# Block sums of a seven-product matmul: from DMAs that add to VectorE with rows loaded aside

## The chip, the cores and the metric

The kernel runs on one core of a Trainium2 chip. The metric is device time in microseconds of one launch. The kernel before took 3009.37 us, the median of three runs (3009.07 to 3009.42).

## The reference, cut to what matters

The program is two transformer blocks in a row, all in fp32, on one sequence of 1024 tokens and a width of 1024. The change touches the last matmul of the first block and what lies beside it:

```python
        gate, up = jnp.split(xn @ w_gate_up[l], 2, axis=-1)
        x = x + (jax.nn.silu(gate) * up) @ w_down[l]
    return rms_norm(x, final_norm_g)
```

`silu(gate) * up` is called h here: 1024 tokens by 2816. `w_down` is 2816 by 1024. Behind it come the norm and the second block, whose context tokens `ctx` (256 by 1024) are normed and modulated on their own.

## The kernel before, in words

Every engine has its own list of instructions, written out in order by a Python function per engine and stage (`down_pe`, `down_act`, `down_dve`, `down_sp`, `down_pool`); each engine works its list strictly in order. `Engine.wait_ge` puts a semaphore wait in front of the next instruction, `did` and `landed` name the event of an instruction or a DMA. The wait holds everything behind it on that engine. SP issues plain loads on its own queue; POOL issues stores, loads and the DMAs that add (`dma_add`), on another queue.

The down product is cut into 2 by 2 blocks and computed with seven block products instead of eight. Names: A is h (`h_dram`, written by the stage before, transposed), A11 to A22 its four blocks, the second digit the half of the inner dimension; B11 to B22 are the blocks of `w_down`. The sums are S1 = A21 + A22, S2 = S1 - A11, S3 = A11 - A21, S4 = A12 - S2, T1 = B12 - B11, T2 = B22 - T1, T3 = B22 - B12, T4 = T2 - B21, up to signs that the results take account of. In the code T1 holds B11 - B12, T2 adds B22 to its source, and so on. `DN_ORDER` is the order of the products: P1 (A11, B11), P2 (A12, B21), P5 (S1, T1), P6 (S2, T2), P7 (S3, T3), P4 (A22, T4), P3 (S4, B22).

Each product has 11 steps, one for each 128 rows of the inner 1408. Step n = 11 * (place in the order) + t runs from 0 to 76 (`dn_step`). A step takes one 128x512 row of A and one of B. ACT writes the rounded high part of each (`dn_highs`), DVE the rest as low part (`dn_lows`), into a ring of four (`hs`, `ws`); ACT waits for PE's step n - 4 before it writes that of step n. PE then does 4 token tiles times 3 matmuls (high-high, high-low, low-high), 12 matmuls of 512 columns, and waits only for the lows of B.

Where the operands of a step lie: for P1, P2, P7 (and A of P4) in rings of eight 128x512 slots, one for A and one for B (`h_slot`, `w_slot`), loaded by SP's `h_ring_load` and `w_ring_load` in the order of use, each waiting until the lows of the slot's user before are made. For P5, P6, P3 and P4's B they lie in two resident buffers of eleven rows, `s_all` (starts as A21) and `t_all` (starts as B12). The block sums turn these in place, S1 to S2 to S4 and T1 to T2 to T4. Here they are all made by DMAs on POOL's queue that add rows from HBM onto what lies in SBUF (`dn_add`), in chunks of 4, 4 and 3 rows; where the sign must turn, ACT first negates the chunk (`dn_negate`). S3 and T3 are made the same way inside the rings, in chunks of 2, 4, 2, 2 and 1 rows. ACT's copies of a step wait for the landing of the add.

Beside this the stage brings back the residual x1 (two halves of the first 512 tokens, then the last 512 tokens, onto `x2`), loads two rows of modulation for the context, loads and norms `ctx` (ACT's squares at step 36, DVE's scaling at step 39, POOL's shift), and DVE adds the products into `x2` (`dn_result`) at the steps that `results` names. `dU2` holds a partial result from step 13 on; `dU3` is free until step 57, but for one row that is scratch of the context's squares. The first transposes of the context (`turn4`) follow step 70 on PE.

## Time and profile before

| | us |
|---|---|
| median of three runs | 3009.37 |
| the profiled execution, its own time | 3012.62 |
| its span, first to last instruction | 3010.80 |
| PE busy | 2828.3 |
| DVE busy | 1795.0 |
| ACT busy | 1352.6 |
| POOL busy | 552.8 |

The profile is of one execution. PE is TensorE's matmuls, PEld its weight loads, DVE is VectorE, ACT ScalarE, POOL GpSimd, SP the engine that issues loads. A row of a timeline is a start, a duration, the engine, the source line (a helper's, the same for many operations), the operation with its operands, how often in a row, and in brackets the idle time before it with what ended it. A window gives busy time and count of each engine, then the granted clock of PE (1.00 is 2.4 GHz, 0.50 is 1.2 GHz), the mean share of the 16 DMA engines, and the rate in GB/s.

### The profile page before, as it was taken

The page shows a single profiled execution, that of the slowest core. Times are in us where ns is not written, and L with a number is a line of the kernel's source. Part 1 is how long each engine was busy: PE and PEld are TensorE (multiplying, and loading weights), DVE is VectorE, ACT ScalarE, POOL GpSimd, SP SyncE. Part 2 cuts the span into 40 slices and gives each one's busy share as a digit, 9 for nine tenths or more (in the row PEclk, how much of TensorE's full clock was granted, in tenths as well). Part 3 has the DMA queues.
Part 4 walks back from the last instruction along what each step waited for, and adds up shares of the span by engine and source line. Part 5 has one row for each costly group of instructions (what it writes and reads, how often), then busy time and mean ns, then how long its engine had stood idle before and what let it go on. Part 6 is the DMA issues. An engine that isn't in the chain of part 4 may idle for free.

```text
span 3010.8 us, 34923 instructions
## 1 busy us (share of the span) xinstructions
PE 2828.3 (94%) x13918; PEld 2247.4 (75%) x13918; DVE 1795.0 (60%) x2506; ACT 1352.6 (45%) x1952; POOL 552.8 (18%) x454
## 2 busy tenths in 40 slices
PE   6999998999999977999999999999999579999997
PEld 5777776788778866888888676666888458888885
DVE  4344534788775446653323555554355669999997
ACT  4344433333333553321111666665213357777775
POOL 0011102555554140332000111111000200000000
PEclk8999999999999988999999999999999789999998
DMA  3210131345654996141221111114324559999996
GB/s 106 84 43 29 43 105 70 99 133 159 184 154 146 309 248 157 39 130 42 68 66 36 49 40 43 39 41 149 105 98 169 223 212 385 398 393 396 397 396 242
DMA packets 258071, 468.65 MB, mean 156 GB/s; under 512 B 28989, under 2 KB 135621, under 8 KB 257397
## 3 DMA queue, kind: packets, MB, share of 16 engines
q1 hardware_dynamic: 223888, 365.46, 34.8%
q0 software_dynamic: 33872, 100.92, 11.6%
q8 instruction: 110, 1.80, 0.3%
q14 instruction: 53, 0.43, 0.0%
q10 hardware_dynamic: 148, 0.04, 0.0%
HBM read 412.79 MB, written 53.58 MB: 155 GB/s over the span
## 4 chain that ended last, share of the span: by engine, by line
PE 85%; DVE 6%; DMA 4%; ACT 3%; issue 2%; POOL 1%; ACTq 0%; POOLq 0%; DVEq 0%
PE PS L130 80%; PE PS L133 5%; DVE m L139 3%; ACT m L136 2%; DMA m<-in_w_down_dram 2%; DVE m L145 1%; DMA m<-h_scratch 1%; DMA m<-in_ctx_dram 1%; ACT L136 0%; DVE m L181 0%; POOL m L139 0%; DVE m L184 0%; DVE m L178 0%; DVE m L148 0%; DMA m<-xh_scratch,small 0%
## 5 line engine op out<-in xcount | busy, mean ns | idle before, releaser
L130 PE MATMUL PS<-m,m 128*128 128x512 f32 (+6 forms) x12102 | 2642.2, 391 | 76.9 <-DVE m L139 55.3
L130 PEld LDWEIGHTS PS<-m,m 128*128 128x128 f32 (+3 forms) x12102 | 2043.7, 185 | 600.2 <-issue 121.3
L136 ACT ACTIVATE m<-m 128x512 fp32r<-128x512 f32 (+5 forms) x739 | 756.4, 1048 | 833.0 <-PE PS L130 402.5
L139 DVE TENSOR_TENSOR m<-m,m 128x512 fp32r<-128x512 f32 (+5 forms) x697 | 882.1, 1292 | 328.7 <-ACT m L136 298.8
L136 ACT ACTIVATE m<-PS 128x512 f32<-128x512 f32 (+4 forms) x507 | 281.9, 578 | 525.7 <-PE PS L130 346.1
L139 DVE TENSOR_TENSOR m<-PS,m 128x512 fp32r<-128x512 f32 (+1 forms) x356 | 233.1, 683 | 346.7 <-PE PS L130 303.7
L139 POOL TENSOR_TENSOR m<-m,m 128x512 f32<-128x512 f32 (+3 forms) x166 | 268.2, 1618 | 584.8 <-DVE small L148 207.9
L133 PE MATMUL PS<-ident,m 128*128 128x128 f32 x1592 | 225.6, 281 | 83.2 <-DVE m L154 36.0
L133 PEld LDWEIGHTS PS<-ident,m 128*128 128x128 f32 x1592 | 193.7, 145 | 122.0 <-DVE m L154 36.2
L136 ACT ACTIVATE m<-m,small 128x640 f32<-128x640 f32 (+4 forms) x199 | 156.3, 788 | 221.1 <-DVE small L142 155.5
L148 DVE CUSTOM_DVE_ANT_0 m<-PS,m 128x640 f32<-128x640 f32 (+4 forms) x192 | 146.4, 775 | 118.6 <-PE PS L130 118.6
L154 DVE COPY m<-PS 128x512 f32<-128x512 f32 (+1 forms) x176 | 106.9, 617 | 134.6 <-PE PS L133 105.8
L145 DVE SCALAR_TENSOR_TENSOR m<-m,small,m 128x512 f32<-128x512 f32 (+1 forms) x155 | 158.5, 1051 | 1.7
L136 ACT ACT_TABLE_LOAD x90 | 115.5, 1283 | 5.5 <-issue 4.0
L145 DVE SCALAR_TENSOR_TENSOR m<-m,vecT,m 128x512 fp32r<-128x512 f32 (+3 forms) x96 | 63.1, 712 | 47.5 <-ACT m L136 46.7
L139 POOL TENSOR_TENSOR m<-m 128x512 f32<-128x512 f32 x52 | 74.8, 1442 | 28.5 <-DMA m<-in_w_gate_up_dram 18.6
L193 POOL DMA_INDIRECT m<-xh_scratch,small x16 | 19.8, 1238 | 304.9 <-PE PS L133 285.3
L193 POOL DMA_INDIRECT xa_scratch<-m,small x15 | 25.5, 1698 | 217.4 <-DVE m L145 217.4
L136 ACT ACTIVATE m<-m,vecT 128x512 fp32r<-128x512 f32 (+2 forms) x80 | 41.2, 598 | 47.2 <-PE PS L130 47.2
L187 POOL DMA_DIRECT2D y_scratch<-m x8 | 4.3, 533 | 259.7 <-DVE m L139 259.7
L139 POOL TENSOR_TENSOR m<-ident,small 128x1024 f32<-128x1024 f32 x16 | 43.3, 2707 | 33.5 <-DVE small L160 33.5
L139 DVE TENSOR_TENSOR small<-small 128x8 f32<-128x8 f32 (+4 forms) x49 | 7.7, 160 | 68.9 <-ACT small L136 63.9
(82 smaller groups left out, 516.5 us busy)
## 6 DMA issues: line engine op xcount, KB each, us to landing
m<-in_w_exp_gate_dram SPq DMA_DIRECT2D x64, 1024.0 KB, 9.2
m<-in_w_exp_up_dram SPq DMA_DIRECT2D x64, 1024.0 KB, 9.3
m<-in_w_exp_down_dram SPq DMA_DIRECT2D x64, 1024.0 KB, 8.8
m<-in_w_mod_dram SPq DMA_DIRECT2D x48, 512.0 KB, 3.8
m<-in_w_gate_up_dram SPq DMA_DIRECT2D x44, 512.0 KB, 6.5
m<-in_w_in_dram SPq DMA_DIRECT2D x41, 512.0 KB, 4.1
m<-in_w_in_dram SPq DMA_DIRECT2D x12, 1024.0 KB, 5.1
h_scratch<-m POOLq DMA_DIRECT2D x22, 512.0 KB, 3.5
```

Of the source, the lines that this page charges most:

```text
L130: return Unsent() if self.e is None else self.e.matmul(o, l, r, start=first, stop=last, **k)
L133: return Unsent() if self.e is None else self.e.transpose(o, i, ident)
L136: return Unsent() if self.e is None else self.e.activation(o, i, fn, **k)
L139: return Unsent() if self.e is None else self.e.tensor_tensor(o, a, b, op)
L145: return Unsent() if self.e is None else self.e.scalar_tensor_tensor(out=o, in0=a, scalar=s, in1=b, op0=op0, op1=op1)
L148: return Unsent() if self.e is None else self.e.tensor_tensor_reduce(**k)
L154: return Unsent() if self.e is None else self.e.tensor_copy(o, i)
L187: return Unsent() if self.e is None else self.e.dma_start(o, i)
L193: return Unsent() if self.e is None else self.e.indirect_dma_start(*a, **k)
```

## The change

Five of the eight sums (T1, S1, S2, S3, T3) are made by DVE, in chunks of 4, 4 and 3 rows, one instruction each (`dn_sum`), at the steps that the new table `sums` names. T1 takes B11 from the ring, where it lies for P1. The other four take their second operand from `dU3`, into which SP loads four rows at a time (`aside_load`, twelve loads); each load waits for the sum before it. The rings hold A11 and B22 for P7 instead of A21 and B12, and from ring entry 22 on the slots are counted two further, so that a chunk of four lies in slots 0 to 3 or 4 to 7. The B ring's loads that overwrite P1's rows wait for T1's sum. T2, T4 and S4 stay DMAs that add. The residual's last part goes to the end of POOL's adds, and its landings are told apart as "first", "second" and "last": `U2_in` waits for "second", `U3_in` and `U3_in0` for "last". The squares' scratch moves from `dU3` to `ar(94, 512)`, with a wait for T3's first sum.

```diff
@@ -1529,15 +1528,20 @@
         dU2, dU3 = ar(134, 4, 512), ar(86, 4, 512)
-        H_RING = [("P1", t, "A11", None) for t in range(11)] + [("P2", t, "A12", None) for t in range(11)] + [
-            ("P7", t, "A21", "A11") for t in range(11)] + [("P4", t, "A22", None) for t in range(11)]
-        W_RING = [("P1", t, "B11", None) for t in range(11)] + [("P2", t, "B21", None) for t in range(11)] + [
-            ("P7", t, "B12", "B22") for t in range(11)]
-
+        H_RING = [(P, t, b) for P, b in (("P1", "A11"), ("P2", "A12"), ("P7", "A11"), ("P4", "A22")) for t in range(11)]
+        W_RING = [(P, t, b) for P, b in (("P1", "B11"), ("P2", "B21"), ("P7", "B22")) for t in range(11)]
         CHUNKS = [(0, 4), (4, 4), (8, 3)]
-        RING_CHUNKS = [(0, 2), (2, 4), (6, 2), (8, 2), (10, 1)]
-        H_AT = {(P, t): j for j, (P, t, b, added) in enumerate(H_RING)}
-        W_AT = {(P, t): j for j, (P, t, b, added) in enumerate(W_RING)}
+
+        def ring_slot(j):
+            return (j if j < 22 else j + 2) % 8
+
+        def ring_before(j):
+
+            users = [i for i in range(j) if ring_slot(i) == ring_slot(j)]
+            return users[-1] if users else None
+
+        H_AT = {(P, t): j for j, (P, t, b) in enumerate(H_RING)}
+        W_AT = {(P, t): j for j, (P, t, b) in enumerate(W_RING)}
         def dn_step(P, t):
             return 11 * DN_ORDER.index(P) + t
@@ -1554,18 +1558,32 @@
             return v.rearrange("(t p) n -> p t n", p=128)
         def h_ring_load(sp, j):
-            P, t, b, _ = H_RING[j]
+            (P, t, b), s_ = H_RING[j], ring_slot(j)
             c = t + 11 * (b[2] == "2")
             sp.wait_ge(f"h_st{c % 2}", c)
-            if j >= 8:
-                sp.wait_ge("h_low", dn_step(*H_RING[j - 8][0:2]), "A")
-            sp.dma_start(h_slot[j % 8], h_block(b, t, 1)).then_inc(*sp.landed(f"h_in{j % 8}", "d", j))
+            if ring_before(j) is not None:
+                sp.wait_ge("h_low", dn_step(*H_RING[ring_before(j)][0:2]), "A")
+            sp.dma_start(h_slot[s_], h_block(b, t, 1)).then_inc(*sp.landed(f"h_in{s_}", "d", j))
         def w_ring_load(sp, j):
-            P, t, b, _ = W_RING[j]
-            if j >= 8:
-                sp.wait_ge("h_low", dn_step(*W_RING[j - 8][0:2]), "B")
-            sp.dma_start(w_slot[j % 8], w_block(b, t, 1)).then_inc(*sp.landed(f"wd_in{j % 8}", "d", j))
+            (P, t, b), s_ = W_RING[j], ring_slot(j)
+            if ring_before(j) is not None:
+                P_, t_, _ = W_RING[ring_before(j)]
+                sp.wait_ge("h_low", dn_step(P_, t_), "B")
+                if P_ == "P1":
+                    sp.wait_ge("x2_half", "T1", t_ // 4)
+            sp.dma_start(w_slot[s_], w_block(b, t, 1)).then_inc(*sp.landed(f"wd_in{s_}", "d", j))
+
+
+        ASIDE = [("S1", 0), ("S1", 1), ("S1", 2), ("S3", 0), ("T3", 0), ("S2", 0), ("S2", 1), ("S2", 2),
+                 ("S3", 1), ("T3", 1), ("S3", 2), ("T3", 2)]
+
+        def aside_load(sp, S, c):
+            n, (t0, m) = ASIDE.index((S, c)), CHUNKS[c]
+            if n:
+                sp.wait_ge("x2_half", *ASIDE[n - 1])
+            src = w_block("B12", t0, m) if S == "T3" else h_block({"S1": "A22", "S2": "A11", "S3": "A21"}[S], t0, m)
+            sp.dma_start(dU3[:, 0:m, :], blocks(src)).then_inc(*sp.landed("cs_raw", S, c))
         def w_last_load(sp, t):
...
@@ -1595,17 +1613,34 @@
             sp.wait_ge("gu_acc", 21, "P7")
             sp.dma_start(t_all, blocks(w_block("B12", 0, 11))).then_inc(*sp.landed("ct_in"))
             for j in range(8, 22):
-                if j == 12:
+                if j == 11:
                     sp.wait_ge("gu_acc", 21, "P4")
                     sp.wait_ge("gu_up", 21, "C12")
                     sp.wait_ge("h_st0", 20)
                     sp.wait_ge("h_st1", 21)
                     sp.dma_start(s_all, blocks(h_block("A21", 0, 11))).then_inc(*sp.landed("cs_raw"))
+                if j in (14, 20):
+                    aside_load(sp, "S1", (14, 20).index(j))
                 h_ring_load(sp, j)
                 w_ring_load(sp, j)
-            for j in range(22, 33):
+            aside_load(sp, "S1", 2)
+            for j in range(22, 26):
                 h_ring_load(sp, j)
                 w_ring_load(sp, j)
+            aside_load(sp, "S3", 0)
+            for j in range(26, 30):
+                h_ring_load(sp, j)
+                w_ring_load(sp, j)
+            aside_load(sp, "T3", 0)
+            for c in range(3):
+                aside_load(sp, "S2", c)
+            aside_load(sp, "S3", 1)
+            aside_load(sp, "T3", 1)
+            aside_load(sp, "S3", 2)
+            for j in range(30, 33):
+                h_ring_load(sp, j)
+                w_ring_load(sp, j)
+            aside_load(sp, "T3", 2)
             for t in range(11):
                 h_ring_load(sp, H_AT["P4", t])
             for t in range(4):
...
@@ -1754,25 +1788,39 @@
                 else:
                     dve.tensor_tensor(L, dn_source(n, x)[0], H.bitcast(F32), ALU.subtract).then_inc(*dve.did("h_low", n, x))
-        def ring_rows(S, c):
-
-            t0, m = RING_CHUNKS[c]
-            ring, at_, sem = (h_ring, H_AT, "h_in") if S == "S3" else (w_ring, W_AT, "wd_in")
-            j = at_["P7", t0]
-            return ring(j % 8, m), [(f"{sem}{(j + a) % 8}", "d", j + a) for a in range(m)]
-
-        def dn_negate(act, S, c):
-
-            if S in ("S3", "T3"):
-                v, ready = ring_rows(S, c)
+        def ring_rows(at_, P, ring, sem, c):
+
+            t0, m = CHUNKS[c]
+            js = [at_[P, t0 + a] for a in range(m)]
+            return ring(ring_slot(js[0]), m), [(f"{sem}{ring_slot(j)}", "d", j) for j in js]
+
+        def dn_sum(dve, S, c):
+
+            t0, m = CHUNKS[c]
+            sv, tv, aside = s_all[:, t0:t0 + m, :], t_all[:, t0:t0 + m, :], dU3[:, 0:m, :]
+            if S == "T1":
+                v, ready = ring_rows(W_AT, "P1", w_ring, "wd_in", c)
+                out_, a, b, op = tv, v, tv, ALU.subtract
+                ready.append(("ct_in",))
+            elif S == "S1":
+                out_, a, b, op, ready = sv, sv, aside, ALU.add, []
+            elif S == "S2":
+                out_, a, b, op, ready = sv, aside, sv, ALU.subtract, [("h_low", dn_step("P5", t0 + m - 1), "A")]
             else:
-                t0, m = CHUNKS[c]
-                v = (s_all if S == "S2" else t_all)[:, t0:t0 + m, :]
-                ready = [{"T1": ("ct_in",), "S2": ("h_low", dn_step("P5", t0 + m - 1), "A"),
-                          "T4": ("h_low", dn_step("P6", t0 + m - 1), "B")}[S]]
+                v, ready = ring_rows(H_AT, "P7", h_ring, "h_in", c) if S == "S3" else ring_rows(W_AT, "P7", w_ring, "wd_in", c)
+                out_, a, b, op = v, v, aside, ALU.subtract
             for event in ready:
-                act.wait_ge(*event)
-            act.activation(v, v, ACT.Copy, scale=-1.0).then_inc(*act.did("dn_neg", S, c))
+                dve.wait_ge(*event)
+            if S != "T1":
+                dve.wait_ge("cs_raw", S, c)
+            dve.tensor_tensor(out_, a, b, op).then_inc(*dve.did("x2_half", S, c))
+
+        def dn_negate(act, c):
+
+            t0, m = CHUNKS[c]
+            v = t_all[:, t0:t0 + m, :]
+            act.wait_ge("h_low", dn_step("P6", t0 + m - 1), "B")
+            act.activation(v, v, ACT.Copy, scale=-1.0).then_inc(*act.did("dn_neg", "T4", c))
         SQ_ORDER = [(0, i) for i in range(4)] + [(1, i) for i in range(4, 8)] + [(0, i) for i in range(4, 8)] + [(1, i) for i in range(4)]
...
@@ -1792,18 +1840,8 @@
         def down_act(act):
             for n in range(4, 77):
                 dn_highs(act, n)
-                if n in (5, 6, 7):
-                    dn_negate(act, "T1", n - 5)
-                if n in (27, 31, 34):
-                    dn_negate(act, "S2", (27, 31, 34).index(n))
                 if n in (38, 42, 45):
-                    dn_negate(act, "T4", (38, 42, 45).index(n))
-                if n in (29, 30, 32):
-                    dn_negate(act, "S3", (29, 30, 32).index(n))
-                    dn_negate(act, "T3", (29, 30, 32).index(n))
-                if n in (47, 48):
-                    dn_negate(act, "S3", n - 44)
-                    dn_negate(act, "T3", n - 44)
+                    dn_negate(act, (38, 42, 45).index(n))
                 if n == 50:
                     w_high(act, W_K2)
                 if n == 13:
@@ -1814,9 +1852,10 @@
                     dn_squares(act, 0, (n - 26, n - 25))
                 if n == 36:
                     act.wait_ge("cx_in")
+                    act.wait_ge("x2_half", "T3", 0)
                     for a in range(2):
                         for z in range(2):
-                            square(act, cx[:, a, half512(z)], ssqc[:, a, z:z + 1], "cx", a, z, junk=dU3[:, 0, :])
+                            square(act, cx[:, a, half512(z)], ssqc[:, a, z:z + 1], "cx", a, z, junk=ar(94, 512))
                 if n == 38:
                     root_of(act, ssumc, "cx")
                 if n in (63, 65):
...
+            sums = {4: ("T1", 0), 5: ("T1", 1), 11: ("T1", 2), 12: ("S1", 0), 15: ("S1", 1), 18: ("S1", 2), 23: ("S3", 0),
+                    25: ("T3", 0), 28: ("S2", 0), 31: ("S2", 1), 34: ("S2", 2), 37: ("S3", 1), 40: ("T3", 1), 48: ("S3", 2), 50: ("T3", 2)}
...
@@ -2035,40 +2068,31 @@
             pool.dma_add(v, blocks(src)).then_inc(*pool.landed(*event))
         def down_pool(pool):
-            pool.wait_ge("h_low", 10, "B")
-            for c in range(3):
-                dn_add(pool, "T1", c)
-                dn_add(pool, "S1", c)
-                if c == 0:
-                    pool.dma_start(x2[:, 0:4, 0:512], x1_dram[0:512, 0:512].rearrange("(i p) n -> p i n", p=128)).then_inc(
-                        *pool.landed("x1_back", "first"))
-            pool.wait_ge("h_low", 22, "B")
+            pool.wait_ge("h_low", 12, "B")
+            pool.dma_start(x2[:, 0:4, 0:512], x1_dram[0:512, 0:512].rearrange("(i p) n -> p i n", p=128)).then_inc(
+                *pool.landed("x1_back", "first"))
             pool.wait_ge("sqrow_a")
+            pool.wait_ge("h_low", 18, "B")
             for dst, j, c in ((cA1row, 1, 1), (csh1row, 1, 0)):
                 row_load(pool, dst, j, c, "crows_in")
-            for c in range(3):
-                dn_add(pool, "T2", c)
-                dn_add(pool, "S2", c)
             pool.wait_ge("x1_back", "first")
             pool.dma_start(cx, ctx_2[0].rearrange("(i p) n -> p i n", p=128)).then_inc(*pool.landed("cx_in"))
             for c in range(3):
-                dn_add(pool, "S3", c)
-                dn_add(pool, "T3", c)
+                dn_add(pool, "T2", c)
             pool.wait_ge("cx_in")
             pool.dma_start(x2[:, 0:4, 512:1024], x1_dram[0:512, 512:1024].rearrange("(i p) n -> p i n", p=128)).then_inc(
-                *pool.landed("x1_back"))
-            pool.dma_start(x2[:, 4:8, :], x1_dram[512:1024, :].rearrange("(i p) n -> p i n", p=128)).then_inc(
-                *pool.landed("x1_back", "last"))
+                *pool.landed("x1_back", "second"))
             for c in range(3):
-                dn_add(pool, "S4", c)
                 dn_add(pool, "T4", c)
                 if c == 0:
                     for a in range(2):
                         pool.wait_ge("cx_scaled", a)
                         pool.tensor_tensor(cx[:, a, :], cx[:, a, :], csh1row, ALU.add).then_inc(*pool.did("cx_shifted", a))
-            for c in (3, 4):
-                dn_add(pool, "S3", c)
-                dn_add(pool, "T3", c)
+            for c in range(3):
+                dn_add(pool, "S4", c)
+            pool.wait_ge("x1_back", "second")
+            pool.dma_start(x2[:, 4:8, :], x1_dram[512:1024, :].rearrange("(i p) n -> p i n", p=128)).then_inc(
+                *pool.landed("x1_back", "last"))
             pool.wait_ge("x2_half", "U3", 3)
             pool.dma_start(sqB, rows_dram[1, 2560:3072].partition_broadcast(128)).then_inc(*pool.landed("sqrow_b"))
             pool.wait_ge("h_low", dn_step("P4", 10), "B")
```

## Rows read from the trace of the kernel before

**Rows 1.** The page: busy time by engine, and the chain by engine.
```profile
PE 2828.3 (94%) x13918; PEld 2247.4 (75%) x13918; DVE 1795.0 (60%) x2506; ACT 1352.6 (45%) x1952; POOL 552.8 (18%) x454
...
PE 85%; DVE 6%; DMA 4%; ACT 3%; issue 2%; POOL 1%; ACTq 0%; POOLq 0%; DVEq 0%
```

**Rows 2.** The chain in order of time: start, us, what.
```profile
1005.41 22.99 DMA m<-in_w_down_dram
...
1121.77 31.50 DMA m<-in_w_down_dram
...
1165.51 43.77 PE PS L130 x192
```

**Rows 3.** Timeline of PE, 965 to 1215: start, us, group, idle time before it.
```profile
970.79 54.65 PE L130 MATMUL PS<-m,m 128*128 128x512 f32 x240 [1.40 <-DVE m L139]
1025.64 3.01 PE L130 MATMUL PS<-m,m 128*128 128x512 f32 x12 [0.20 <-DVE m L139]
1029.83 33.26 PE L130 MATMUL PS<-m,m 128*128 128x512 f32 x144 [1.17 <-DVE m L139]
1066.08 12.81 PE L130 MATMUL PS<-m,m 128*128 128x512 f32 x48 [2.99 <-DVE m L139]
1089.20 11.01 PE L130 MATMUL PS<-m,m 128*128 128x512 f32 x36 [10.31 <-DVE m L139]
1102.76 33.32 PE L130 MATMUL PS<-m,m 128*128 128x512 f32 x144 [2.54 <-DVE m L139]
1154.70 54.58 PE L130 MATMUL PS<-m,m 128*128 128x512 f32 x228 [18.63 <-DVE m L139]
1209.12 0.60 PE L133 MATMUL PS<-ident,m 128*128 128x128 f32 x4
```

**Rows 4.** Timeline of ACT, 1170 to 1179: two splits with nothing late.
```profile
1171.29 1.15 ACT L136 ACTIVATE m<-m 128x512 fp32r<-128x512 f32 x2 [1.57 <-PE PS L130]
1174.01 1.16 ACT L136 ACTIVATE m<-m 128x512 fp32r<-128x512 f32 x2 [1.57 <-PE PS L130]
```

**Rows 5.** Windows of 5 us, then the stage: busy by engine, PEclk, DMA share, GB/s.
```profile
1145.00:1150.00 5.00, 0.00 (x0) 0.00 (x0) 0.00 (x0) 0.00 (x0) 0.00 (x0) 0.50 1.13 207
...
985.00:990.00 5.00, 5.00 (x24) 4.14 (x23) 2.50 (x4) 5.00 (x6) 0.00 (x0) 1.00 1.05 388
1030.00:1035.00 5.00, 5.00 (x23) 4.12 (x24) 5.00 (x9) 3.33 (x7) 1.16 (x2) 1.00 1.10 257
970.00:1210.00 240.00, 203.21 (x858) 164.68 (x859) 129.54 (x212) 122.36 (x201) 51.29 (x43) 0.92 0.93 240
```

**Rows 6.** DMA issues in narrow windows, then the page: KB each, us to landing.
```profile
m<-h_scratch SPq DMA_DIRECT2D x1, 256.0 KB, 3.0
...
m<-in_w_down_dram SPq DMA_DIRECT2D x1, 2816.0 KB, 16.4
...
m<-in_w_down_dram SPq DMA_DIRECT2D x1, 256.0 KB, 22.5
...
m<-in_w_in_dram SPq DMA_DIRECT2D x12, 1024.0 KB, 5.1
```

**Rows 7.** Timeline of SP's queue near 1002: one issue and how long it took.
```profile
1001.73 1.87 SPq L187 DMA_DIRECT2D m<-in_w_down_dram  x1
```

**Rows 8.** Timeline of ACT, 1055 to 1090: its wait ahead of the context's squares.
```profile
1084.32 0.63 ACT L136 ACTIVATE m<-m 128x512 f32<-128x512 f32 x1 [14.60 <-DMA m<-in_ctx_dram]
```

**Rows 9.** Timeline of ACT and of DVE, 970 to 1000: splits and the first negation.
```profile
976.58 1.15 ACT L136 ACTIVATE m<-m 128x512 fp32r<-128x512 f32 x2 [1.57 <-PE PS L130]
982.45 10.30 ACT L136 ACTIVATE m<-m 128x2048 f32<-128x2048 f32 x13 [4.71 <-DMA m<-in_w_down_dram]
...
977.25 1.29 DVE L139 TENSOR_TENSOR m<-m,m 128x512 fp32r<-128x512 f32 x2 [1.43 <-ACT m L136]
```

**Rows 10.** Groups of DVE by form, 970 to 1210: busy, mean ns, idle before.
```profile
L139 DVE TENSOR_TENSOR m<-m,m 128x512 fp32r<-128x512 f32 x135 | 92.4, 727 | 109.0 <-ACT m L136 108.5
...
L139 DVE TENSOR_TENSOR m<-m,m 128x2048 fp32r<-128x2048 f32 x1 | 2.3, 2292 | 0.9 <-ACT m L136 0.9
```

More of the change, by code:

```diff
@@ L1917, in dn_result @@
                     dve.wait_ge("x2_half", "U2", i)
-                    dve.wait_ge("x1_back", "last")
+                    dve.wait_ge("x1_back", "second")
                     xs = x2[:, i, half512(1)]
@@ L1952, in down_dve @@
                 dn_lows(dve, n)
+                if n in sums:
+                    dn_sum(dve, *sums[n])
                 if n in results:
```

31 lines of the change are left out of this document (10 added, 21 removed), and 2 rows, old and new, of the table SHARED.

## The prediction

> **What bounds the kernel now.** I read the shares first: PE is busy 94% of the span and the chain that ended last runs over PE for 85% [rows 1], so time comes only from holes in PE's row or from a lower clock. The long pieces of the chain that are not PE lie almost all between 1005 and 1153 us, and they are DMAs into the down product's operands [rows 2]. PE's own timeline there [rows 3] shows what they cost. The product has 77 steps of 12 matmuls, and from step 4 ACT's splits for a step begin when PE has ended the step four before it; two such splits in the undisturbed part are 2.72 us apart [rows 4], so a step is 2.72 us. Step 0 starts at 970.79, and the first transposes, which follow step 70, at 1209.12. 71 steps at 2.72 are 193.1 us, 238.3 were used: 45.2 us are lost. 35.8 of them are PE waits (0.20+1.17+2.99+10.31+2.54+18.63). Most of the other 9.4 is the clock: behind the 2.99 us wait, 48 matmuls took 12.81 instead of 10.9 us, behind the 10.31 us wait 36 took 11.01 instead of 8.2, behind the 18.63 us wait 19 steps took 54.6 instead of 51.7 [rows 3].
>
> Why the DMAs are late is in the windows [rows 5]: the engines' share is full in all three, but they move 388 GB/s of plain loads, 257 with adds mixed in, 207 where only adds are left. Ring loads of 256 KB, which take 3.0 us on an empty queue, take 22.5 [rows 6]; SP gets rid of one each 1.87 us [rows 7], that is 262 KB/1.87 = 140 GB/s for its queue beside 117 for the adds.
>
> **The change part by part.** I give T(n), the start of step n on PE, and follow it through. The splits' lows of step n (two DVE instructions, 1.3 us) end about 1.9 us after T(n-3) where nothing disturbs, 6.2 us before T(n).
>
> *What goes:* 19 of POOL's 28 adds (T1, S1, S2 three each, S3 and T3 five each; T2, T4, S4 keep nine) and 16 of ACT's 19 negations. T1, 2.9 MB, needs no further load, since B11 already lies in the ring; S1, S2, S3, T3 load 11.5 MB aside by plain DMAs. So 14.4 MB less are added at 207 GB/s (70 us of full engines) and 11.5 MB more loaded at 388 (30 us). The stage's mean DMA share is 0.93 over 240 us [rows 5]; where the engines are full the windows show 1.05 to 1.13, so some 203 us of full engines become 163 in a stage of some 205. The ring loads should then land in time, and all six waits and their clock go: up to -45.2 us. ctx and the residual no longer stand behind several adds; ACT's 14.60 us wait for ctx [rows 8] goes.
>
> *First new cost, the start.* DVE's T1 sum of chunk 0 sits behind the lows of step 4 and waits for t_all, which lands when ACT's wait for it ends now, 982.45 [rows 9] (16.4 us behind its issue [rows 6]). Behind it in DVE's order are the lows of step 5, now made at 977.25 [rows 9]. Sum 2.3 us (the 128x2048 form [rows 10]), lows 1.3: T(5) is 986.05 where 984.4 was due, +1.65. The second sum comes next, then the lows of 6: 989.65 where 988.8 was due, +0.9. Together 2.5. SP's load W 8 now waits for the first sum too, and everything behind it in SP's order (H 9 on, s_all, the rings up to 15) starts at 984.8 and not at 969. From there all is first in, first out: W 8 to W 10 1.3 MB, s_all 2.9, rings 11 to 13 1.6, first aside 1.05. Data run from 987.1 (the 3.0 us of a lone load less its 0.7 us of data), so the first aside lands at 987.1 + 6.8/0.388 = 1004.7. Its sum stands behind lows 12. The rule for all sums: a sum of four rows (2.3) and the next lows (1.3) must end by T(n+1), so the aside has to be there by T(n) - 0.9. T(12) is 1006.0: it is on time, at no cost.
>
> *The second aside (S1, chunk 1)* is queued behind the rings 14 to 19, 3.1 MB, and shares the engines with the first part of the residual (1.05 MB, issued at lows 12): 1004.7 + (3.15 + 1.05 + 1.05)/0.388 = 1018. T(15) is 1014.15, so it was due at 1013.2. DVE waits, nothing behind it runs, T(16) becomes 1018+2.3+1.3 = 1021.6 instead of 1016.9: +4.7, and by the 2.99 us wait's example about +1.9 for the clock. This is the largest single term; bounds 0 (landing 5 us sooner) and 12 (at the mixed 257 GB/s it lands at 1025).
>
> *The other asides.* Each is issued when the sum before it ends, three steps (8.2 us) apart, and DVE has some 6 us in hand. A lone 1 MB load lands in 5.1 us [rows 6]; beside a busy add queue it is 1.05/0.140 + 2.3 = 9.8 us. Following the chain: S1 chunk 2, S3 0 and T3 0 hide (their neighbours are plain loads; landings 1024.7, 1036.6, 1044.8 against T(18), T(23), T(25) of 1027, 1040.6, 1046.1, so T3 0 is the closest). S2 0 is issued at 1047.1 beside the first T2 add, lands at 1055.4 (5 us at 0.140 beside the add, the rest at 0.388), due 1053.4: +2.0. S2 1: +0.4. S2 2: 0. S3 1 shares with the last T2 add and the second part of the residual: +0.6. T3 1, beside the first T4 add and behind DVE's cx scaling (2.5 us): +1.3. S3 2 has four steps of room: 0. T3 2 is issued when S3 2's sum ends (1109.7), lands beside S4's adds at 1117.6, and DVE still has W_K2's low (2.3 us) ahead of lows 51: +1.7. Together 6.0; bounds 0 (each lone, 5.1) and 27 (nine rounds of 9.8+2.3 are 109 us, less the 28 steps from 12 to 40, 76, less 6 in hand).
>
> Where DMA's queues meet, the Trainium skill (DMA: Bandwidth & Descriptors, section Queues, rings and completion order) says that each DMA engine takes turns between the queues it has work for, a packet at a time. The trace agrees (140 beside 117 GB/s [rows 5, 7]). By that rule one queued add is enough to hold an aside to 9.8 us; without it the term would be 0 and the time 6 us less. That all nine meet an add is the first rival.
>
> *At nothing:* DVE's 31.5 us of sums (11 rows x 5 x 0.57) lie in its idle time: it waits 109.0 us for ACT in this stage [rows 10]. ACT's negations of the remaining T4 are unchanged. POOL waits, behind the first T4 add, for DVE's cx scaling (about 1089) and then adds the shift; T4's other two, S4's three and the residual's last part are queued behind that, and still have ten and more steps before P4 (step 55) and P3 (step 66). C11 at step 24 wants the residual's first part, issued at lows 12 and landed by 1012; ACT's new wait at step 36 for T3's first sum (1047) is long met, so nothing queues behind it. The residual's last 2 MB now come after S4, by some 1133, wanted at step 58 (about 1142). The ring's wait for step 44 to 46 leaves S3 2 landing at 1108, wanted by T(48) - 0.9 = 1112.
>
> *Sum:* 45.2 - 2.5 - 6.6 - 6.0 = 30.1 us less. The profiled execution took 3012.62 (span 3010.80 and 1.82 around it): 2982.5. The median shown, 3009.37, is 3.25 below it: 2979.3, so 2979.
>
> **Rivals.** *Every round meets adds:* 27 instead of 6 for the asides: 3009.4 - 45.2 + 2.5 + 6.6 + 27 = 3000. For: 9 adds, the second and last parts of the residual, ctx and the rows share this stretch. Against: the first four rounds are over before T2's first add. *Every aside hides:* only the start costs, 3009.4 - 45.2 + 2.5 = 2967. For: DMA share falls by a quarter. Against: the second aside's place behind twelve ring loads. *Slower, by DVE's order:* DVE waits in order, in front of every lows behind it, for loads that stand in SP's queue behind ring loads. If asides land as ring loads do now (22.5), nine rounds take 9 x 24.8 = 223, less 76 and 6: 141 lost, against 45.2 - 2.5 - 6.6 = 36.1 gained: 3009.4 + 141 - 36.1 = 3114. It decides from a mean of 10.8 us for an aside (nine rounds of 13.1 are 118, less 82, are 36); mine is 7 us. For: the traced 22.5. Against: that number is made by the adds that go. *Nothing comes through:* the holes close and a later stage waits instead, 3009. For: little; from 1165 on the chain is PE again, in one piece of 43.77 us [rows 2].
>
> **How the numbers follow.** Forecast (2970 to 2989) 0.60; every aside hides 0.17; adds meet every round (2989 to 3005) 0.13; nothing comes through 0.04; slower 0.06. About 0.2% (6 us) is what can be told from no change. Faster 0.89, of the adds' case a little falls within 0.2%: same 0.05, slower 0.06. The range, 2966 to 2998, takes the best case and most of the third.
>
> **What would show it.** DVE's L139 gains 15 instructions of 128x2048 and 128x1536 in the stage; PE's waits there fall from 37.2 in all (35.8 and the 1.40 ahead of step 0 [rows 3]) to about 15, the longest near 1017 and of 4 to 5 us, with a half clock right behind; two short ones near 984 and 989; ACT's wait for ctx is gone; the first transposes behind step 70 come near 1179 instead of 1209. Ring loads land in under 12 us from 1010 on. Wrong it would be by a wait over 8 us anywhere, by T2, T4 or S4 adds landing later than their product, or by DVE waits for asides that repeat every third step at more than 3 us.

## The result, and the profile after

The changed kernel takes 2993.9 us, the median of five runs (2991.9 to 2995.9), against 3009.42 for the kernel before, again of five (3009.07 to 3010.84): ratio 0.9947, 95% interval 0.9933 to 0.9962, 15.5 us or 0.5% faster. Forecast were 2979 us and 30 us. The direction held and the time lies in the stated range of 2966 to 2998, but not in the part of it that was forecast (2970 to 2989, given 0.60): it lies in the one given 0.13. The size came to half.

The page of the kernel after: busy time by engine, and the chain by engine.

```profile
PE 2824.4 (94%) x13918; PEld 2243.3 (75%) x13918; DVE 1825.1 (61%) x2521; ACT 1332.8 (45%) x1936; POOL 529.8 (18%) x435
...
PE 83%; DVE 8%; DMA 4%; ACT 2%; issue 2%; POOL 1%; SPq 0%; ACTq 0%; POOLq 0%; DVEq 0%
```

Against [rows 1] PE is busy 3.9 us less with the same 13918 matmuls, and the chain runs over DVE for 8% instead of 6, with DMA still at 4: the new sums stand on it, and the loads that they wait for.

PE's timeline of the stage, kernel after; it answers to [rows 3].

```profile
971.27 13.89 PE L129 MATMUL PS<-m,m 128*128 128x512 f32 x60 [1.40 <-DVE m L138]
986.66 3.04 PE L129 MATMUL PS<-m,m 128*128 128x512 f32 x12 [1.50 <-DVE m L138]
990.07 13.89 PE L129 MATMUL PS<-m,m 128*128 128x512 f32 x60 [0.37 <-DVE m L138]
1006.37 15.48 PE L129 MATMUL PS<-m,m 128*128 128x512 f32 x60 [2.40 <-ACT m L135]
1024.90 24.94 PE L129 MATMUL PS<-m,m 128*128 128x512 f32 x108 [3.05 <-DVE m L138]
1050.42 3.06 PE L129 MATMUL PS<-m,m 128*128 128x512 f32 x12 [0.58 <-DVE m L138]
1054.73 8.48 PE L129 MATMUL PS<-m,m 128*128 128x512 f32 x36 [1.25 <-DVE m L138]
1065.59 30.61 PE L129 MATMUL PS<-m,m 128*128 128x512 f32 x132 [2.39 <-DVE m L138]
1099.78 33.08 PE L129 MATMUL PS<-m,m 128*128 128x512 f32 x132 [3.57 <-DVE m L138]
1135.86 56.64 PE L129 MATMUL PS<-m,m 128*128 128x512 f32 x240 [3.00 <-DVE m L138]
1192.33 0.60 PE L132 MATMUL PS<-ident,m 128*128 128x128 f32 x4
```

The counts divided by 12 give the steps: waits ahead of steps 5, 6, 11, 16, 25, 26, 29, 40 and 51. In [rows 3] they are ahead of steps 20, 21, 33, 37, 40 and 52, so the one at step 40 is in both. The nine sum to 18.1 us, where [rows 3] has 35.8; the longest is 3.57 instead of 18.63. From step 0 to the first transposes it is 1192.33 - 971.27 = 221.1 us, where 238.3 were used before. The ideal is still 193.1, so 27.9 us are lost now: 18.1 in waits, 9.8 in clock and in the ends of groups (12 matmuls alone take 3.04 us where a step takes 2.72, so about 0.3 us an end). The forecast had left 15.1.

Windows of the kernel after (busy and count of PE, PEld, DVE, ACT, POOL, then granted clock, DMA share, GB/s), beside [rows 5].

```profile
980.00:985.00 5.00, 5.00 (x23) 3.94 (x21) 1.88 (x1) 2.12 (x4) 0.00 (x0) 1.00 0.36 140
1005.00:1010.00 5.00, 3.63 (x9) 2.95 (x10) 2.62 (x2) 3.90 (x8) 0.78 (x1) 0.66 1.06 388
1025.00:1030.00 5.00, 5.00 (x22) 4.14 (x23) 3.88 (x5) 1.15 (x2) 1.76 (x3) 1.00 0.91 312
1065.00:1070.00 5.00, 4.41 (x19) 3.68 (x20) 4.22 (x10) 1.16 (x2) 1.30 (x1) 1.00 0.97 263
1100.00:1105.00 5.00, 5.00 (x12) 3.91 (x13) 5.00 (x7) 2.71 (x3) 1.29 (x1) 0.50 0.29 68
1135.00:1140.00 5.00, 4.14 (x11) 3.29 (x12) 4.42 (x8) 0.14 (x1) 0.00 (x0) 0.66 1.10 289
```

The first row is new: the DMA engines stand mostly idle at 980 to 985, because SP waits at the B ring's entry 8. Plain loads still move 388 GB/s (1005). In the rows at 1005, 1100 and 1135 the granted clock is 0.66, 0.50 and 0.66, that is partly or wholly the 1.2 GHz level, right behind the waits at steps 11, 40 and 51; behind those at steps 16 and 29 (1025, 1065) it stays at 2.4 GHz.

DVE's waits, kernel after, 970 to 1210: for whom, us in total, times, longest. Before, 108.5 of DVE's 109.0 us of idle time ahead of its splits were for ACT [rows 10].

```profile
DVE m L138 <- ACT m L135: 27.5, 21, 6.1
DVE m L138 <- DMA m<-h_scratch: 26.2, 8, 7.6
DVE m L138 <- DMA m<-in_w_down_dram: 13.1, 3, 6.8
```

DVE's timeline, kernel after: rows with a sum that waited for an aside, and the stretch around the context's scaling.

```profile
983.12 10.52 DVE L138 TENSOR_TENSOR m<-m,m 128x2048 f32<-128x2048 f32 x12 [6.78 <-DMA m<-in_w_down_dram]
...
1021.35 5.91 DVE L138 TENSOR_TENSOR m<-m,m 128x2048 f32<-128x2048 f32 x7 [7.63 <-DMA m<-h_scratch]
...
1062.05 3.49 DVE L138 TENSOR_TENSOR m<-m,m 128x2048 f32<-128x2048 f32 x3 [3.73 <-DMA m<-h_scratch]
...
1086.62 2.29 DVE L138 TENSOR_TENSOR m<-m,m 128x2048 f32<-128x2048 f32 x1 [3.93 <-DMA m<-h_scratch]
...
1094.09 11.45 DVE L138 TENSOR_TENSOR m<-m,m 128x512 fp32r<-128x512 f32 x9
...
1130.64 8.78 DVE L138 TENSOR_TENSOR m<-m,m 128x1536 f32<-128x1536 f32 x10 [5.52 <-DMA m<-in_w_down_dram]
```

The 7.63 us ahead of 1021.35 is the second aside, the 3.73 and 3.93 us are for S2's first and S3's second aside, the 5.52 us is for the last of T3. ACT's wait for ctx [rows 8] is gone, as forecast.

### The profile page after: what moved, and what is told of

It reads as the page before. It is cut to its first block, busy times and chain, and to the rows that moved or that the text cites. A ratio compares the mean times of both kernels' runs of the same rounds, so it can differ in the third digit from the quotient of the medians.

```text
span 2990.1 us, 34923 instructions
## 1 busy us (share of the span) xinstructions
PE 2824.4 (94%) x13918; PEld 2243.3 (75%) x13918; DVE 1825.1 (61%) x2521; ACT 1332.8 (45%) x1936; POOL 529.8 (18%) x435
## 4 chain that ended last, share of the span: by engine, by line
PE 83%; DVE 8%; DMA 4%; ACT 2%; issue 2%; POOL 1%; SPq 0%; ACTq 0%; POOLq 0%; DVEq 0%
PE PS L129 78%; PE PS L132 5%; DVE m L138 4%; DMA m<-h_scratch 2%; ACT m L135 2%; DVE m L144 1%; DMA m<-in_w_down_dram 1%; POOL m L138 1%; ACT L135 0%; DVE m L180 0%; DVE m L183 0%; DVE m L177 0%; DVE m L147 0%; SPq L186 0%; DVE m L141 0%
## 5 line engine op out<-in xcount | busy, mean ns | idle before, releaser
L135 ACT ACTIVATE m<-m 128x512 fp32r<-128x512 f32 (+5 forms) x723 | 736.8, 1041 | 831.5 <-PE PS L129 434.9
L138 DVE TENSOR_TENSOR m<-m,m 128x512 fp32r<-128x512 f32 (+7 forms) x712 | 912.5, 1312 | 283.1 <-ACT m L135 214.4
```

The source lines that it names most:

```text
L135: return Unsent() if self.e is None else self.e.activation(o, i, fn, **k)
L138: return Unsent() if self.e is None else self.e.tensor_tensor(o, a, b, op)
```

## The experiments

Twelve runs, in three groups, each beside the kernel before: order, copy12, cxlate, two; tiny, plain, combo, best; changed, thin, noshift, hold. "Stage" is PE's time from step 0 to the first transposes in the run's profile, "waits" PE's in it (the 1.40 us ahead of step 0 left out), "other loss" what the stage has above 193.1 us beside them, the ratio is to the kernel before in the same group.

| kernel | median us | ratio (95%) | stage | waits | other loss |
|---|---|---|---|---|---|
| before | 3009.4 | | 238.3 | 35.8 | 9.4 |
| after | 2993.9 | 0.9947 (0.9933 to 0.9962) | 221.1 | 18.1 | 9.8 |
| changed (after, again) | 2994.2 | 0.9950 (0.9932 to 0.9967) | 224.8 | 21.2 | 10.4 |
| tiny | 2968.3 | 0.9862 (0.9846 to 0.9879) | 200.6 | 4.7 | 2.8 |
| plain | 2971.9 | 0.9878 (0.9861 to 0.9894) | 203.2 | 5.8 | 4.4 |
| order | 2987.4 | 0.9929 (0.9912 to 0.9946) | 217.3 | 14.5 | 9.6 |
| copy12 | 2992.5 | 0.9948 (0.9931 to 0.9964) | 223.6 | 21.1 | 9.4 |
| cxlate | 2990.6 | 0.9943 (0.9926 to 0.9959) | 222.4 | 17.8 | 11.4 |
| noshift | 2991.4 | 0.9939 (0.9922 to 0.9957) | 221.3 | 16.7 | 11.5 |
| hold | 2986.8 | 0.9929 (0.9912 to 0.9947) | 217.3 | 13.7 | 10.4 |
| thin | 2975.1 | 0.9892 (0.9874 to 0.9909) | 204.6 | 7.5 | 4.0 |
| two | 2979.4 | 0.9903 (0.9886 to 0.9919) | 210.0 | 10.5 | 6.3 |
| combo | 2972.3 | 0.9879 (0.9862 to 0.9895) | 205.7 | 7.8 | 4.8 |
| best | 2973.7 | 0.9884 (0.9867 to 0.9900) | 204.2 | 6.5 | 4.7 |

### What the adds cost the kernel before: tiny and plain

```diff
-            pool.dma_add(v, blocks(src)).then_inc(*pool.landed(*event))
+            pool.dma_add(v[0:16, 0:1, :], blocks(src)[0:16, 0:1, :]).then_inc(*pool.landed(*event))   # tiny
+            pool.dma_start(v, blocks(src)).then_inc(*pool.landed(*event))                             # plain
```

tiny: 

> The kernel before with each of its 28 adding DMAs cut to 16 partitions of one row; all waits, negations and ring loads are as before, but the block sums are not formed, so that part of the product is left out. My theory: the adds' bytes are what cost the kernel before its 45.2 us in this stage. Without them PE's waits are under 4 us in all, step 0 to the first transposes takes 194 to 199 us instead of 238.3, and the median is 39 to 45 us lower. Rival: the order of waits (negate, add, copy on three queues) costs as such; then over 10 us of PE waits stay and the gain is under 32.

plain: 

> The kernel before with its 28 adding DMAs made plain loads of the same rows to the same places on the same queue, so the sums are replaced by their second operand and the product is not the reference's. My theory: what hurts is that an added byte takes the DMA engines 1.9 times as long as a loaded one (207 against 388 GB/s); 23 MB take 59 us and not 111, the engines are no longer full, PE's waits fall from 37 to 5 to 15 us and the median is 25 to 38 us lower. Rival: it is the number of bytes and POOL's queue being first in, first out (ctx and residual behind the adds); then over 20 us of waits stay and the gain is under 20 us.

PE's timeline of plain.

```profile
1025.84 54.92 PE L130 MATMUL PS<-m,m 128*128 128x512 f32 x240 [0.77 <-DVE m L139]
1085.74 87.88 PE L130 MATMUL PS<-m,m 128*128 128x512 f32 x372 [4.98 <-DVE m L139]
1173.45 0.60 PE L133 MATMUL PS<-ident,m 128*128 128x128 f32 x4
```

Both came out as my theory had it in the median; tiny kept a wait of 4.74 us at step 40 and took 200.6 us of stage where I had said under 4 and 194 to 199. With every byte still moved on the same queues, but loaded instead of added, the stage falls from 238.3 to 203.2. So 35 of the 45 us were the rate of the adds, and only 2.6 more are had by not moving the bytes at all. The order of negation, transfer and copy over three queues is not what cost.

What is left there is not the adds' either. The wait of 4.74 and 4.98 us is at step 40 in both, where [rows 3] has 2.54. Two of DVE's splits, 1.29 us where nothing disturbs, come there right behind the context's scaling, while POOL adds the shift to the context, and take 5.52 us in tiny and 5.51 in plain. In the kernel before they had taken as long, in its chain of work:

```profile
1097.13 5.58 DVE m L139 x2
```

So this wait was never the adds' alone; cxlate and noshift below act on it.

### How steady the changed kernel is: changed

> The changed kernel once more, as the measure for the three beside it: median 2991 to 2995, step 0 to the first transposes 220 to 223 us (221.1 in its first profile), PE's waits at the same steps 5, 6, 11, 16, 25, 26, 29, 40 and 51.

The median is the same within 0.4 us, but the stage of this profile took 224.8, above what I expected, and not all waits are at the same steps: none at 25 and 26, small ones at 38, 41 and 49. The wait at step 51 was 6.21 us here and 3.00 in the first. The chain of work of this profile shows from where:

```profile
1112.08 10.57 DMA m<-h_scratch
```

This is the last ring load of A11, which S3's last sum needs; in the first profile it took 6.1 us. The last aside waits for that sum. It took 10.2 us in both profiles, but was issued at 1124.6 here and at 1120.4 there. A single profile's stage is good to some 4 us, and differences under that are read from waits and not from the sum.

### The start of the stage: order and copy12

```diff
-            for j in range(8, 22):
-                if j == 11:
+            for j in range(8, 12):
+                h_ring_load(sp, j)
...
+            sp.dma_start(s_all, blocks(h_block("A21", 0, 11))).then_inc(*sp.landed("cs_raw"))
+            for j in range(8, 12):
+                w_ring_load(sp, j)
+            for j in range(12, 22):
```

order: 

> The changed kernel, but SP issues H 8 to H 11 and the 2.9 MB load of s_all ahead of W 8, which is the load that waits for the first T1 sum; W 8 to W 11 follow. Nothing else differs. My theory: in the changed kernel the waits at step 11 (2.40 us, and the half clock behind it) and at step 16 (3.05 us) come from loads that stand behind W 8 while the DMA engines are at a share of 0.36 (980 to 985). With s_all issued at 981 instead of 988 all that follows lands 5 us or more sooner: both waits shrink or go, the stage from step 0 to the first transposes takes 214 to 217 us instead of 221.1, the median is 2986 to 2990. Rival: the aside for S1 chunk 1 is late because of the bytes ahead of it and not because of when they start; then the wait at step 16 stays near 3 us and the median stays within 1.5 us of 2993.9.

PE's timeline of order.

```profile
989.98 27.54 PE L129 MATMUL PS<-m,m 128*128 128x512 f32 x120 [0.37 <-DVE m L138]
1018.77 22.06 PE L129 MATMUL PS<-m,m 128*128 128x512 f32 x96 [1.25 <-DVE m L138]
...
1188.32 0.60 PE L132 MATMUL PS<-ident,m 128*128 128x128 f32 x4
```

The wait at step 11 is gone (steps 6 to 15 are one group of 120) and that at step 16 is 1.25 instead of 3.05, with full clock in between; the median came as the theory had it, the stage 0.3 us above its range. The four runs (2986.0 to 2987.9) lie below all of the changed kernel's. At 980 to 985 the DMA engines' share is 1.05 now, where it was 0.36. The loads were late because they started late.

```diff
-                if n == 13:
+                if n == 12:
                     for i in range(4):
                         act.wait_ge("dn_acc", 10, i)
```

copy12: 

> The changed kernel, but ACT copies P1's result out of PSUM behind the splits of step 12, not of step 13. My theory: PE's 2.40 us wait at step 11 is for these copies, which stand behind the splits of step 13, and these wait for ring entry 13. Here that wait goes with its half clock (4 us). But the aside for S1 chunk 1 lands when it lands (1021), whatever PE does, so PE's wait at step 16 grows by about as much as was gained, from 3.05 to some 7 us, and the median moves by less than 2 us. Rival: the two waits are independent, and the median falls by 4 us, to 2990.

The stretch that it is about, first in the kernel after (all engines), then PE's in copy12.

```profile
1003.07 2.67 ACT L135 ACTIVATE m<-m 128x512 fp32r<-128x512 f32 x4 [1.23 <-DMA m<-h_scratch]
...
1005.65 2.04 ACT L135 ACTIVATE m<-PS 128x512 f32<-128x512 f32 x4
...
1006.37 5.96 PE L129 MATMUL PS<-m,m 128*128 128x512 f32 x18 [2.40 <-ACT m L135]
```

```profile
1004.32 5.72 PE L129 MATMUL PS<-m,m 128*128 128x512 f32 x24 [0.16 <-ACT m L135]
1010.67 8.46 PE L129 MATMUL PS<-m,m 128*128 128x512 f32 x36 [0.64 <-DVE m L138]
1024.23 28.86 PE L129 MATMUL PS<-m,m 128*128 128x512 f32 x120 [5.10 <-DVE m L138]
```

After: ACT makes the splits of steps 12 and 13 (the four from 1003.07, held up by the ring's landings) and only then copies P1 out of PSUM at 1005.65; PE's step 11 starts 0.7 us behind the first copy. In copy12 that wait is 0.16 us. But the wait at step 16 has grown from 3.05 to 5.10 (I had said some 7) with 0.64 at step 13, and the median is the same within its noise: the aside lands when it lands.

### Step 40: cxlate and noshift

```diff
                 if n == 39:
                     inverse_of(dve, ssumc, rsc, "cx")
+                if n == 53:
                     dve.wait_ge("rstd", "cx")
...
-                if c == 0:
-                    for a in range(2):
-                        pool.wait_ge("cx_scaled", a)
-                        pool.tensor_tensor(cx[:, a, :], cx[:, a, :], csh1row, ALU.add).then_inc(*pool.did("cx_shifted", a))
...
                 *pool.landed("x1_back", "last"))
+            for a in range(2):
+                pool.wait_ge("cx_scaled", a)
+                pool.tensor_tensor(cx[:, a, :], cx[:, a, :], csh1row, ALU.add).then_inc(*pool.did("cx_shifted", a))
```

cxlate: 

> The changed kernel, but DVE's scaling of the context comes at step 53 instead of 39, and POOL's shift of it behind the residual's last load. My theory: PE's wait of 3.57 us at step 40 and the half clock behind it come from DVE being full there: the sum S3 chunk 1, the scaling (2.5 us) and then nine instructions that take 11.45 us instead of some 7 while POOL adds the shift. With both moved to where DVE has room the wait is under 1 us and the median 5 to 7 us lower, 2987 to 2989. Rival: the wait is from the asides of S3 and T3 chunk 1 alone, which landed at 1086.6; then it stays over 2 us and the median falls by under 2 us.

In noshift the shift keeps its place and is cut:

```diff
-                        pool.tensor_tensor(cx[:, a, :], cx[:, a, :], csh1row, ALU.add).then_inc(*pool.did("cx_shifted", a))
+                        pool.tensor_tensor(cx[:, a, 0:8], cx[:, a, 0:8], csh1row[:, 0:8], ALU.add).then_inc(*pool.did("cx_shifted", a))
```

noshift: 

> The changed kernel with POOL's shift of the context cut to 8 of 1024 columns, DVE's work and every wait as they were; the context's shift is left out but for those columns. My theory: DVE's nine instructions behind the scaling took 11.45 us beside POOL's 6.1 us of adding and not 7.1 as they do alone, and these 4.3 us stand in PE's wait of 3.57 us at step 40. Here they take 7.1 us, the wait at step 40 is under 0.5 us with no half clock behind it, the stage is 3 to 6 us shorter; part comes back as a longer wait at step 51, as it did when scaling and shift came later. Rival: the nine instructions are slow for another reason; then they still take over 10 us.

DVE's timeline of cxlate: the nine instructions that are the stretch at 1094.09 in the kernel after, now alone; eight that meet the shift; and eight alone.

```profile
1097.91 7.11 DVE L138 TENSOR_TENSOR m<-m,m 128x2048 f32<-128x2048 f32 x9 [5.56 <-DMA m<-in_w_down_dram]
...
1140.00 9.30 DVE L138 TENSOR_TENSOR m<-m,m 128x512 fp32r<-128x512 f32 x8
...
1151.62 4.89 DVE L138 TENSOR_TENSOR m<-m,m 128x512 fp32r<-128x512 f32 x8
```

The mechanism is there: the nine instructions take 7.11 us instead of 11.45, and where the shift now runs eight of 512 columns take 9.30 us where eight alone take 4.89. noshift shows the same 7.11. But removing it alone gives little back. In both kernels the wait at step 40 went and one of 2.0 us stands at step 41, where T3's second aside is not there yet, and the wait at step 51 is 4.5 and 5.4. The stage is no shorter than the changed kernel's. I had expected a median 5 to 7 us lower of cxlate and a stage 3 to 6 us shorter of noshift; the median of cxlate (2990.6) lies between what its theory and its rival gave, and by the ratios it is some 1 us below the changed kernel. Removing one of two causes that stand one behind the other brought out the second.

### Step 51: hold

```diff
-            for c in range(3):
-                dn_add(pool, "S4", c)
             pool.wait_ge("x1_back", "second")
             pool.dma_start(x2[:, 4:8, :], x1_dram[512:1024, :].rearrange("(i p) n -> p i n", p=128)).then_inc(
                 *pool.landed("x1_back", "last"))
+            pool.wait_ge("x2_half", "T3", 2)
+            for c in range(3):
+                dn_add(pool, "S4", c)
```

> The changed kernel with POOL's last four issues in another order: the residual's last part first, then S4's three adds, which also wait for the last T3 sum. My theory: the aside of T3 chunk 2 takes some 10 us because S4's adds (2.9 MB) are in flight beside it; with them held back it lands in 6 to 8 us, the wait of 3.00 us at step 51 falls under 1.5 us with its half clock, the median is 2 to 4 us lower. Rival: it is late because the load is issued late (behind S3 chunk 2's sum) and the residual's 2 MB take the adds' place beside it; then the wait at step 51 stays over 2.5 us.

The wait at step 51 is 0.28 us, in place of 3.00 and 6.21. The median is 7.4 us below that of the changed kernel in the same group, more than expected. The last aside lands in 7.0 us instead of 10.2, and S3's last sum, ahead of it, waits 0.39 us for its ring load where it waited 4.41 in changed. So the adds made both late, and the residual's plain load in their place did no harm.

### DVE's own time, and two buffers: thin and two

```diff
-            dve.tensor_tensor(out_, a, b, op).then_inc(*dve.did("x2_half", S, c))
+            dve.tensor_tensor(out_[:, :, 0:8], a[:, :, 0:8], b[:, :, 0:8], op).then_inc(*dve.did("x2_half", S, c))   # thin
```

thin: 

> The changed kernel with DVE's fifteen block sums cut to 8 of 512 columns; waits, loads and order stay, the sums are not formed. My theory: DVE's time for the sums (31.5 us) is not the cost, but each late aside makes PE wait for landing + 2.3 + 1.3 us, so cutting the sums shortens each late round by up to 2.2 us and gives 8 to 14 us of the 27.9 lost; PE waits at steps 11 and 16 stay over half. Rival: DVE is the bound of the stage; then nearly all waits go and the stage takes 193 to 200 us, 21 us or more less.

PE's timeline of thin.

```profile
1004.35 15.33 PE L129 MATMUL PS<-m,m 128*128 128x512 f32 x60 [2.25 <-ACT m L135]
1020.76 27.49 PE L129 MATMUL PS<-m,m 128*128 128x512 f32 x120 [1.09 <-DVE m L138]
...
1090.01 30.50 PE L129 MATMUL PS<-m,m 128*128 128x512 f32 x132 [2.39 <-DVE m L138]
...
1176.53 0.60 PE L132 MATMUL PS<-ident,m 128*128 128x128 f32 x4
```

The stage fell by 16.5 us against the first profile after and 20.1 against the second, the median by 19.1 in the same group: more than my theory gave, just short of the rival. The wait at step 11 stayed (2.25 us), that at step 16 fell to 1.09 against what I expected. But DVE was not full in the kernel after: there it waits 39.3 us for DMAs and 27.5 for ACT, and in thin 50.5 for DMAs. What the sums' time does, as I read it, is to stand in the round: an aside is issued when the sum before it ends, so landing, 2.3 us of sum and the next issue follow one another, and three steps are 8.2 us long. Without the 2.3 us the rounds nearly fit.

```diff
+        aside_at = [dU3, shaped(piece(32, 2048, F32), (4, 512))]
...
-            if n:
-                sp.wait_ge("x2_half", *ASIDE[n - 1])
+            if n >= 2:
+                sp.wait_ge("x2_half", *ASIDE[n - 2])
...
-            sp.dma_start(dU3[:, 0:m, :], blocks(src)).then_inc(*sp.landed("cs_raw", S, c))
+            sp.dma_start(aside_at[n % 2][:, 0:m, :], blocks(src)).then_inc(*sp.landed(("cs_raw", "cs_odd")[n % 2], S, c))
```

The rest of this edit follows from it: `dn_sum` reads the buffer in turn, and W_K2's split comes at step 52, behind T3's last sum.

two: 

> The changed kernel with two buffers for the rows aside, used in turn, so that each load waits for the sum before the last one; W_K2's split, whose place the second buffer borrows, comes at step 52 instead of 50. My theory: DVE's waits for asides (39 us in all, 11 times) come from a load being issued only when the sum before it has ended. With two buffers PE's waits at steps 25, 26, 29 and 51 (0.58, 1.25, 2.39, 3.00) and most of that at 40 go, the stage is 8 to 12 us shorter, the median 2982 to 2987. Rival: the loads are slow because the engines are shared with the adds, so that issuing them sooner only makes them take longer; then the median falls by under 3 us.

PE's timeline of two.

```profile
1005.22 15.23 PE L129 MATMUL PS<-m,m 128*128 128x512 f32 x60 [3.03 <-ACT m L135]
1023.75 29.13 PE L129 MATMUL PS<-m,m 128*128 128x512 f32 x120 [3.30 <-DVE m L138]
1053.35 38.38 PE L129 MATMUL PS<-m,m 128*128 128x512 f32 x168 [0.47 <-DVE m L138]
1092.75 3.02 PE L129 MATMUL PS<-m,m 128*128 128x512 f32 x12 [1.02 <-DVE m L138]
1096.15 52.84 PE L129 MATMUL PS<-m,m 128*128 128x512 f32 x228 [0.38 <-DVE m L138]
1149.58 30.22 PE L129 MATMUL PS<-m,m 128*128 128x512 f32 x132 [0.58 <-DVE m L138]
```

The sums are whole again here. The waits behind step 25 are 0.47, 1.02, 0.38 and 0.58 instead of 0.58, 1.25, 2.39, 3.57 and 3.00, and the stage is 11.1 us shorter, as expected; the median, 2979.4, is 2.6 us below what I expected. Those at steps 11 and 16 did not shrink. The rival falls: issued sooner, the loads did land sooner, and DVE's waits for DMAs fell from 39.3 to 26.8 us.

### Together: combo and best

combo: 

> The changed kernel with three edits together: two buffers for the rows aside, H 8 to H 11 and s_all issued ahead of W 8, and P1's copies behind the splits of step 12. My theory: the waits at steps 11 and 16 that two buffers alone left (3.03 and 3.30 us, with a half clock between) are those that the other two edits act on, and with the bytes there in time they go now: stage 202 to 205 us instead of 209.95 with two buffers alone, the median 5 to 7 us below that kernel's 2979.4. Rival: they do not add up, since each only moves the wait on to the next aside; then the median is within 3 us of 2979.4.

best, with `{5: ("T1", 0), 6: ("T1", 1)` in place of `{4: ("T1", 0), 5: ("T1", 1)`: 

> The kernel of the run before this one, and the first two T1 sums on DVE one step later (behind the lows of steps 5 and 6). My theory: the lows of step 5 no longer stand behind the wait for t_all (983.1), and PE's waits at steps 5 and 6 (1.35 and 0.39 us) go, 1.5 us of median, at no cost, because W 8 was released by the landing of t_all and not by the sum's place. Rival: the lows of step 6 and 7 now take the wait; then the stage is the same within 0.5 us.

PE's timeline of combo.

```profile
971.13 13.88 PE L129 MATMUL PS<-m,m 128*128 128x512 f32 x60 [1.40 <-DVE m L138]
...
1019.67 29.11 PE L129 MATMUL PS<-m,m 128*128 128x512 f32 x120 [2.03 <-DVE m L138]
1050.00 38.38 PE L129 MATMUL PS<-m,m 128*128 128x512 f32 x168 [1.22 <-DVE m L138]
...
1176.87 0.60 PE L132 MATMUL PS<-ident,m 128*128 128x128 f32 x4
```

The waits at steps 11 and 16 have become one of 2.03 at step 16, and the median is 2972.3: 36 us below the kernel before, and by the ratios (0.9879 and 0.9947, intervals apart) some 20 us below the changed kernel. It is 7.1 us below two as well, so the rival that the edits do not add up falls; the stage is 0.7 us above what I expected. In best the waits at steps 5 and 6 are gone, but one of 2.17 stands at step 8; its stage is 1.5 us shorter than combo's and its median 1.4 us longer, so no gain can be claimed for that edit.

## Why the prediction was right and where it was off

*What bounds the kernel, and that the adds are the cause:* right in the main. Of the 45.2 us lost in the stage, plain shows 35 to be the adds' rate, and tiny 38 the adds' in all. ACT's wait for ctx went, and five of the six old waits. The sum counted all six as gone. The one at step 40 stayed (2.54 before, 3.57 after): POOL's shift has its part in it, and the change leaves the shift as it was.

*The start (+2.5):* 1.50 + 0.37 measured, where forecast (steps 5 and 6). *The second aside (+4.7):* its load took 11.2 us from issue to landing, about 11 forecast, and the wait is where it was said to be. The first aside had landed at 1007.8 and not at 1004.7, so this one was issued some 3 us later, at 1010.1. It is 3.05 us and not 4.7, because PE came later to it: the 2.40 us at step 11 were not in my sum. I had named what the T1 wait holds up on SP's queue and checked the landings against the splits of their own step, and not against what stands behind the splits on ACT: P1's copies, for which PE's step 11 waits. copy12 shows that this error cost nothing clear of noise in the total: its step 16 starts at 1024.23, against 1024.90.

*The other asides (+6.0):* the term that was mis-sized most in waits. 10.8 us were measured at steps 25, 26, 29, 40 and 51. The rounds were sized nearly rightly (the last nine asides took a mean of 7.4 us, where 7 was said; S2's first took 8.4 where 8.3 was forecast, the next 5.5 where 6.3 was), but two things were left out. S3's first aside took 11.4 where 7.7 was forecast, behind ring loads and with ctx and the rows on the other queue. And at step 40 DVE's instructions take longer while POOL adds, 4.3 us over nine of them by cxlate. The trace of the kernel before could have told it, in a row of DVE's timeline that I had not used:

```profile
1097.05 10.81 DVE L139 TENSOR_TENSOR m<-m,m 128x512 fp32r<-128x512 f32 x10
```

Ten splits in 10.81 us, where two take 1.29; POOL's shift ran beside the first of them. The term has an error the other way too: its due times from step 18 on leave out the 1.9 us of clock that the sum then adds, and with it in, the 2.0 us for S2's first aside would be nearly nothing.

*The clock (+1.9):* the largest error in size. The prediction charged one half clock, behind the second aside. It came behind three waits, at steps 11, 40 and 51, and together with the ends of the groups 9.8 us are lost beside the waits, as many as before (9.4), though the longest wait is a fifth as long. In the sum I had let all 9.4 us go with the old waits and put back 1.9. Some 2.6 of the 9.8 us are the ends of nine groups, at 0.3 us each; the rest, some 7, is clock. A stage with nine short waits pays nearly the same for the clock as one with six, of which two were long. thin, combo and best, with five to eight waits of 2.4 us at most, lose 4.0 to 4.8 there.

So the step that failed is the sum's last line: 15.1 us put back, 27.9 measured. Of the 12.8 between, 7.9 are clock and ends of groups and 4.9 are waits. That the time still lies in the range is not to the sum's credit: the range had been drawn to take in most of the rival's case. The rival "every round meets adds" (3000) comes nearer in time than my forecast, but not in mechanism: the asides of S2, S3 and T3 took from 4.9 to 11.4 us. The longest, S3's first, met no add at all, but ring loads, ctx and the rows; three of 7.4 to 8.4 and the last, of 10.2, ran beside adds; two others that an add joined took 5.3 and 5.5. two and hold show that it was the issue behind the sum, and at the end the adds, and not nine rounds of 9.8 us.

Left open: which part of the round's cost the ring loads bear, since no run had asides without them; why the last ring load of A11 took 6.1 us in one profile and 10.6 in the other; and what the shift at step 40 costs once the asides are in time, since no run has two buffers and leaves it out.

## What to carry to other kernels

Here the DMAs that add moved 207 GB/s where loads moved 388, and what shared the engines with them came late too; as DVE had idle time, loading the operand aside and summing there gave part of that back. But a single buffer turned it into a round of landing, sum and next issue on an engine that works in order. Compare the round with the distance of its uses, and try a second buffer first: of the single edits that keep the result, it brought the most (some 13 us by the ratios). When waits are forecast, price the clock for short ones too, and look behind the late instruction on its own engine, not only at its reader. And before a wait is counted as gained, ask of each one what made it: one of the six here had a second cause that stayed.

## What the runs showed of the hardware

Plain loads from HBM moved 388 GB/s and adding ones 207, with the 16 engines' share full in both [rows 5], and two queues in use shared the engines about evenly (140 and 117 GB/s [rows 5, 7]). DVE's instructions on two operands in SBUF are slowed by POOL's adds: eight DVE instructions of 128x512 took 9.30 us beside POOL's shift, 4.89 alone (cxlate). PE's clock fell to half behind a wait of 2.40 us (step 11) and not behind one of 3.05 (step 16) or 2.39 (step 29) in the same profile. In changed, the second profile of this kernel, it was at half behind a wait of 3.10 us at step 16 (0.50 at 1026 to 1030), and at full behind one of 3.60 at step 40 (1.00 at 1101 to 1103), where the first profile has half behind 3.57. The length of the last wait alone doesn't tell it.
